# Expert weights of a two-layer mixture-of-experts kernel: fourteen places of 1 MB filled by a table, in place of a ring of seven places of 2 MB

## The chip, the cores and the metric

The kernel runs on 1 core of one Trainium2 chip. The metric is the device time of one execution in microseconds (us); three runs of the kernel before gave 3231.19 us in the median. A core has a matrix engine (TensorE, PE in the profile), a vector engine (DVE), a scalar engine (ACT), GpSimd (POOL), and a sync engine (SP) that here only waits and issues DMAs; 16 DMA engines carry what any of them issues.

## The reference, cut to what matters

Two transformer blocks follow each other over 1024 tokens of width 1024, all in float32. Each ends in a mixture of experts: 32 experts, every token goes to 2, each expert has three weight matrices of 2 MB.

```python
def expert_block(args):
    xb, e = args
    return (jax.nn.silu(xb @ w_gate[e]) * (xb @ w_up[e])) @ w_down[e]
```

`w_gate[e]` and `w_up[e]` are 1024x512, `w_down[e]` is 512x1024. The outputs are weighted by the router and summed per token. Everything else (attention of two kinds, gating, norms) is not touched by the change, apart from renamed semaphores.

## The kernel before, in words

The kernel is written engine by engine: one Python function per stage and engine, and semaphores between them. The two expert stages are the calls with L = 0 and L = 1 of `sync_experts`, `tensor_experts` and their siblings.

**Blocks.** The kernel sorts the tokens of a layer by expert and the experts by load, and has a fixed plan: `PROFILE` says how many rows the expert of each rank gets at most, `ORDER` in which order the ranks come. Class `Plan` (L1389) makes a list of blocks of 64 or 32 rows out of it. An expert has one to four blocks: in layer 0 there are 51 blocks (37 of 64 rows and 14 of 32), in layer 1 46 (36 and 10). Positions 0, 6 and 17 of layer 0 and position 16 of layer 1 have four blocks of 64 rows; positions 10 and 21 of layer 0 and 3 and 11 of layer 1 have three. 31 experts stand in the plan; whatever overflows goes through a hardware loop (`sync_loop`, `tensor_loop`), which here runs once in each layer, ahead of position 27 in layer 0 and 26 in layer 1.

**Weights.** SP loads `w_gate`, `w_up` and `w_down` of one expert after the other, in one DMA of 2 MB each (`load_expert`, L1763 and L1766). Load number n goes into place n % 7 (`RING`), seven places of 2 MB in SBUF. Before it issues, SP waits (`freed`) until the last block of the expert that held the place is through its product: `p_gu` counts the blocks whose gate and up products are done, `p_dn` those whose down product is done. SP works strictly in this order; a load that waits holds back all behind it. A load of gate or up brings 16 KB in one piece to each of 128 partitions, a load of down four pieces of 4 KB.

**Products.** For block b TensorE does four of the eight steps kk of the gate and up products (L1667), then the transposes of the hidden rows of block b - 1 (L1622) and of the next tokens (L1613), then the other four steps (L1667 again), then the down product of block b - 1 (L1640). So the down product of an expert's last block comes behind the gate and up products of the next expert's first block. At an expert's first block it waits for gate and up together (`weight`), at its first down product for down.

Beside the weights the DMA engines carry, for each block, the token rows that GpSimd gathers (`rows_in`) and the output rows that it stores (`rows_out`).

Of the kernel before, what the change touches and what calls it, by code (L numbers as in the profile page):

```python
# [85 lines left out]
class Shared:  # L86
# [7 lines left out]
    "d_gate d_attn d_q0 d_q1 d_row d_rowb d_dil d_norm0 d_norm1 d_post "  # L94
    "a_cond v_acc p_col v_mod "
    "a_sq v_rstd v_xn p_tr v_tr a_tr "
    "z_q p_in v_in a_in "
    "v_ln a_ln p_ws v_ws p_sv "
# [3 lines left out]
    "d_zero d_wr d_xn0 d_xn1 p_lg v_rt a_rt p_cnt p_tab "  # L102
    "d_e0 d_e1 d_e2 d_e3 d_e4 d_e5 d_e6 d_xt0 d_xt1 d_xt2 d_xt3 d_xt4 d_ys0 d_ys1 d_ys2 d_ys3 d_ys4 d_ys5 "
    "p_xt v_xt a_xt p_gu a_sg v_h p_ht v_ht p_dn v_yb v_gh "
# [390 lines left out]
def vector_gate(k):  # L495
    V, s = k.nc.vector, k.s
# [20 lines left out]
    V.wait_ge(s["p_ws"].sem, 1)  # L517
# [3 lines left out]
    for m in range(NT):  # L521
        V.wait_ge(s["p_sv"].sem, m + 1)
# [21 lines left out]
def tensor_gate_weights(k):  # L544
# [5 lines left out]
    i_.then_inc(*s["p_ws"].up())  # L550
# [66 lines left out]
def sync_attn(k):  # L617
    Q, s, A = k.nc.sync, k.s, k.A
    v = attn_views(k)
    d = s["d_attn"]  # L620
    Q.wait_ge(s["v_ws"].sem, 17)
    Q.wait_ge(s["p_sv"].sem, 8)
# [9 lines left out]
def vector_attn(k):  # L632
# [3 lines left out]
    V.wait_ge(s["p_sv"].sem, 8)  # L636
    V.memset(v.relp, 0.0).then_inc(*pr.up())
    V.wait_ge(s["d_attn"].sem, 400)
# [58 lines left out]
def scalar_attn(k):  # L697
# [4 lines left out]
    S.wait_ge(s["p_sv"].sem, 8)  # L702
# [432 lines left out]
def vector_route(k, L, scale, bias, biased):  # L1135
# [82 lines left out]
    V.wait_ge(s["p_cnt"].sem, L + 1)  # L1218
# [66 lines left out]
    V.wait_ge(s["p_tab"].sem, L + 1)  # L1285
# [35 lines left out]
def tensor_route(k, L):  # L1321
# [34 lines left out]
    i_.then_inc(*s["p_tab"].up())  # L1356
# [27 lines left out]
RING = 7  # L1384
# [7 lines left out]
class Plan:  # L1392
# [3 lines left out]
    def __init__(self, profile, firsts, before):  # L1396
# [25 lines left out]
        self.loop_at = tuple((3 * self.loop_q + j) % RING for j in range(3))  # L1422
        self.b0, self.t0, self.w0 = (0, 0, [0] * RING) if before is None else (
            before.b0 + len(before.blocks), before.t0 + len(before.tiles),
            [before.loads(u, 10 ** 9) for u in range(RING)])

    def number(self, q, j):


        return 3 * (q + (q >= self.loop_q)) + j  # L1430

    def loads(self, u, n):

        return self.w0[u] + len([m for m in range(u, 96, RING) if m <= n and m // 3 != self.loop_q])

# [11 lines left out]
def expert_views(k):  # L1447
    v = Shared()
    ring = [k.R2[:, 4096 * u:4096 * u + 4096] for u in range(4)]
    ring += [k.R0[:, 4096 * u:4096 * u + 4096] for u in range(2)]  # L1450
    ring.append(k.R1[:, 0:4096])
    v.flat = ring
    v.up = [r.rearrange("p (k n) -> p k n", k=8) for r in ring]
    v.down = [r.rearrange("p (k n) -> p k n", k=4) for r in ring]
# [146 lines left out]
def tensor_experts(k, L):  # L1601
# [14 lines left out]
    def hidden_T(b):  # L1616
# [4 lines left out]
        for kk in range(P.blocks[b].rows // 16):  # L1621
            i_ = T.transpose(k.ps[:, hidden_bank(b), 64 * kk:64 * kk + 64], v.hb[:, 128 * kk:128 * kk + 128],  # L1622
                             k.ident[0:64, 0:64])
# [144 lines left out]

# [975 lines left out]
```

## Time and profile before

| | us |
|---|---|
| median of 3 runs | 3231.19 (3224.49 to 3260.21) |
| span of the profiled execution | 3229.6 |
| PE busy | 2768.7 (86%) |
| DVE, ACT, POOL busy | 1130.5, 646.7, 304.5 |
| chain that ended last: PE | 74% |
| chain that ended last: DMA | 13%, of it the load of w_up 8% and of w_down 2% |
| bytes by DMA | 605.18 MB, mean 187 GB/s |

The chain is followed back from the last instruction, at each step to what released it. Busy is the time in which an engine executes; the share of DMA in a window is the mean over the 16 engines. The first expert stage lies between 934 and 1622 us of the span, the second between 2540 and 3180 us.

### The profile page before, as it was taken

Reading aid. Unit: us, or ns where it says so; the run is one execution under the profiler, and the core shown is the slowest. Engines: PE = TensorE matmul, PEld = TensorE weight load, DVE = VectorE, ACT = ScalarE, POOL = GpSimd, SP = SyncE. Lnnn points to the kernel's source line nnn. Section 1 sums busy time; section 2 is a strip of 40 time slices with the busy share of each in tenths; the row PEclk is TensorE's granted clock in tenths of the full one; section 3 lists DMA queues with packets and bytes.
Section 4 is the critical chain, followed back from the end, with each engine's and each line's share of the span. In section 5 each row is a group of like instructions: output and inputs, shape, how many; then the busy total and the mean of one; then the engine's idle time right before and its main releaser. Section 6 shows DMA issues by size and latency. Waiting matters only on the chain.

```text
span 3229.6 us, 34694 instructions
## 1 busy us (share of the span) xinstructions
PE 2768.7 (86%) x13500; PEld 1352.3 (42%) x13500; DVE 1130.5 (35%) x2847; ACT 646.7 (20%) x1603; POOL 304.5 (9%) x395
## 2 busy tenths in 40 slices
PE   3999999998949878978659999999998489888972
PEld 2456844444443333333224444555564433333421
DVE  4225724337462112211160002777723612111214
ACT  3115600000111101100041001555612111111101
POOL 0000000000001101111020000222500111111102
PEclk9999999999969989989879999999989689989996
DMA  7221014227156988899952100000000699898997
GB/s 272 104 72 53 2 52 156 86 97 247 42 221 232 353 330 333 305 343 370 352 194 97 52 26 1 27 27 28 26 2 20 231 340 385 309 369 304 369 388 276
DMA packets 193830, 605.18 MB, mean 187 GB/s; under 512 B 53122, under 2 KB 95618, under 8 KB 177156
## 3 DMA queue, kind: packets, MB, share of 16 engines
q1 hardware_dynamic: 137076, 531.35, 43.6%
q0 software_dynamic: 56592, 71.62, 6.9%
q8 instruction: 108, 1.77, 0.2%
q14 instruction: 54, 0.44, 0.0%
HBM read 554.65 MB, written 47.98 MB: 187 GB/s over the span
## 4 chain that ended last, share of the span: by engine, by line
PE 74%; DMA 13%; DVE 9%; issue 2%; ACT 1%; SPq 0%; POOL 0%; DVEq 0%; POOLq 0%; ACTq 0%
PE ps L1667 17%; DMA R<-in_w_up 8%; PE ps L1640 7%; PE ps L928 7%; PE ps L2184 6%; PE ps L2616 3%; PE ps L2181 3%; PE ps L433 3%; PE ps L932 3%; PE ps L1046 3%; PE ps L439 2%; DMA R<-in_w_down 2%; PE ps L2425 2%; PE ps L1613 2%; PE ps L2429 1%
## 5 line engine op out<-in xcount | busy, mean ns | idle before, releaser
L1667 PE MATMUL ps<-R 128*64 128x512 f32 (+1 forms) x3872 | 675.4, 549 | 151.6 <-DMA R<-in_w_up 110.0
L1667 PEld LDWEIGHTS ps<-R 128*64 128x64 f32 (+1 forms) x3872 | 221.9, 135 | 525.1 <-issue 490.9
L1640 PE MATMUL ps<-R 128*64 128x512 f32 (+1 forms) x1936 | 309.7, 509 | 2.2 <-DVE R L1504 2.2
L928 PE MATMUL ps<-R 128*128 128x512 f32 x512 | 227.5, 604 | 0.5 <-ACT R L723 0.5
L1567 ACT ACTIVATE R<-ps,small 128x64 f32<-128x64 f32 (+1 forms) x256 | 87.3, 421 | 684.2 <-PE ps L1613 684.2
L2184 PE MATMUL ps<-R 128*128 128x512 f32 x512 | 220.5, 592 | 1.6 <-DVE R L2006 1.6
L1504 DVE COPY R<-ps 128x256 f32<-128x256 f32 (+1 forms) x97 | 37.9, 391 | 450.2 <-PE ps L1622 450.2
L1640 PEld LDWEIGHTS ps<-R 128*64 128x64 f32 (+1 forms) x1936 | 106.3, 126 | 189.1 <-issue 171.7
L1532 DVE TENSOR_TENSOR R<-ps,R 64x512 f32<-64x512 f32 (+1 forms) x97 | 59.8, 617 | 313.7 <-PE ps L1667 201.2
L928 PEld LDWEIGHTS ps<-R 128*128 128x128 f32 x512 | 98.8, 194 | 124.5 <-issue 123.8
L2184 PEld LDWEIGHTS ps<-R 128*128 128x128 f32 x512 | 97.0, 190 | 122.8 <-issue 121.0
L1581 ACT ACTIVATE R<-ps 64x512 f32<-64x512 f32 (+1 forms) x97 | 52.5, 541 | 472.8 <-PE ps L1667 472.7
L1692 POOL DMA_INDIRECT R<-XN,xidx x52 | 52.3, 1006 | 812.5 <-DVE R L1292 794.2
L1046 PE MATMUL ps<-R 128*128 128x512 f32 x256 | 116.3, 617 | 0.0
L2616 PE MATMUL ps<-R 128*128 128x512 f32 x256 | 113.0, 604 | 0.4 <-DVE R L2303 0.4
L433 PE MATMUL ps<-R 128*128 128x512 f32 x256 | 110.2, 592 | 0.0
L2181 PE MATMUL ps<-R 128*128 128x512 f32 x256 | 110.2, 592 | 0.0
L887 DVE TENSOR_TENSOR XR<-ps,XR 128x512 f32<-128x512 f32 x32 | 22.0, 691 | 214.0 <-PE ps L932 214.0
L1495 DVE TENSOR_SCALAR R<-ps,small 128x64 f32<-128x64 f32 (+1 forms) x256 | 75.9, 359 | 40.7 <-PE ps L1613 40.0
L1699 POOL DMA_DIRECT2D YE<-R x49 | 39.4, 805 | 522.1 <-DVE R L1516 504.2
L2425 PE MATMUL ps<-R,cst 128*128 128x512 f32 (+3 forms) x192 | 80.5, 501 | 1.4 <-DVE R L2340 1.4
L905 ACT ACTIVATE XR<-ps 128x512 f32<-128x512 f32 x32 | 19.1, 597 | 309.1 <-PE ps L928 309.1
(320 smaller groups left out, 3586.9 us busy)
## 6 DMA issues: line engine op xcount, KB each, us to landing
R<-in_w_gate SPq DMA_DIRECT2D x64, 2048.0 KB, 17.5
R<-in_w_up SPq DMA_DIRECT2D x64, 2048.0 KB, 18.4
R<-in_w_down SPq DMA_DIRECT2D x64, 2048.0 KB, 24.7
R<-in_w_ada SPq DMA_DIRECT2D x40, 1024.0 KB, 5.4
R<-in_w_in SPq DMA_DIRECT2D x13, 2048.0 KB, 9.2
YE<-R POOLq DMA_DIRECT2D x41, 256.0 KB, 21.7
R<-in_w_ada SPq DMA_DIRECT2D x4, 2048.0 KB, 16.4
XR<-in_x SPq DMA_DIRECT2D x16, 512.0 KB, 11.5
```

The lines of the kernel that those rows point to most:

```text
L433: i_ = T.matmul(k.ps[:, b, :], wv[:, kk, 128 * a:128 * a + 128], toks, start=kk == 0, stop=kk == 7)
L928: i_ = T.matmul(o, wv[:, kk, cols], k.hT[:, kk, tk], start=kk == 0, stop=kk == 7)
L932: i_ = T.matmul(o, w4[:, g, cols], x4[:, g, tk], start=g == 0, stop=g == 3)
L1046: i_ = T.matmul(k.ps[:, n % 6, :], lhsT[:, m, 128 * i:128 * i + 128], wv[:, m, :], start=m == 0, stop=m == 7)
L1495: i_ = V.tensor_scalar(v.xT[t % 2][:, kk, 0:n], k.ps[:, 2, 128 * kk:128 * kk + n], scale[:, kk:kk + 1], bias[:, kk:kk + 1], ALU.mult, ALU.add)
L1567: i_ = S.activation(v.xT[t % 2][:, 4 + kk, 0:n], k.ps[:, 3, 128 * kk:128 * kk + n], ACT.Identity, scale=scale[:, 4 + kk:5 + kk], bias=bias ...
L1640: i_ = T.matmul(k.ps[r * j:r * j + r, 5 + b % 2, 0:n], v.hT[b % 2][:, c:c + r], v.down[m][:, kk, n * j:n * j + n], start=kk == 0, stop=kk ...
L1667: i_ = T.matmul(k.ps[P0 + r * j:P0 + r * j + r, b % 2, 0:n], x_, w[:, kk, n * j:n * j + n], start=kk == 0, stop=kk == 7)
L2181: i_ = T.matmul(k.ps[:, second_bank(n), :], k.hT[:, kk, 128 * x:128 * x + 128], wv[:, kk, :], start=kk == 0, stop=kk == 7)
L2184: i_ = T.matmul(k.ps[:, second_bank(n), :], wv[:, kk, 128 * x:128 * x + 128], k.hT[:, kk, 512 * hf:512 * hf + 512], start=kk == 0, stop=kk ...
L2425: i_ = T.matmul(z, k.C("nge"), lp[:, 0:N], start=False, stop=first and not diag, skip_group_check=True)
L2616: i_ = T.matmul(k.ps[:, 2 * (n % 3) + a, :], v.oT[a][:, c, 128 * i:128 * i + 128], w[4 * a + c][:, 512 * h2:512 * h2 + 512], start=c == 0, ...
```

## The change

Each weight matrix is cut into two halves of 1 MB, and SBUF holds them in 14 places (`HOMES`) that fill the same bytes as the seven did. An expert has six parts, loaded as gate and up of the first half (parts 0, 1), gate and up of the second half (2, 3), and the two halves of down (4, 5). A half of gate or up holds the rows of four of the eight steps kk, a half of down those of two of its four; each half is 8 KB in one piece to each partition. Which place a part takes is fixed when the program is built: `products` lists the order of the products, and `place_pieces` gives each part the place whose present content is used up first by that list. A new semaphore `p_g0` counts the blocks whose first four steps of gate and up are done.

```diff
+    def place_pieces(self):
+        last = {what: n for n, what in enumerate(self.products())}
...
+        for q in names:
+            for part in range(6):
+                u = min(range(HOMES), key=lambda u: (until[u], u))
+                self.home[q, part], self.held[q, part] = u, held[u]
+                held[u], until[u] = (q, part), last[q, (0, 0, 1, 1, 2, 2)[part]]
```

```diff
-    def freed(n):
-
-        q, j = (n - RING) // 3, (n - RING) % 3
-        if n >= RING and q != P.loop_q:
-            q -= q > P.loop_q
-            Q.wait_ge(s["p_dn" if j == 2 else "p_gu"].sem, P.b0 + P.ends[q])
+    def freed(q, part):
+        if P.held[q, part] is not None:
+            q0, part0 = P.held[q, part]
+            if q0 != "loop":
+                Q.wait_ge(s[("p_g0", "p_g0", "p_gu", "p_gu", "p_dn", "p_dn")[part0]].sem, P.b0 + P.ends[q0])
...
+def load_piece(k, part, weights, e_r, place, sem, by):
+    w, half = (weights[part % 2], part // 2) if part < 4 else (weights[2], part - 4)
+    src = w.rearrange("e (p k) n -> e p (k n)", p=128)[:, :, 2048 * half:2048 * half + 2048]
+    k.nc.sync.dma_start(place, src[bass.ds(e_r, 1), :, :].rearrange("o p n -> (o p) n")).then_inc(sem, by)
```

Since down is now loaded with rows 4p to 4p+3 on partition p (so that a half is one piece), the hidden values have to come in the same order. For blocks of 64 rows the transposes of the hidden rows read every fourth element; for blocks of 32 rows the gate and up products read their weights two elements of each four, and the transposes every second element.

```diff
-            if first:
-                weight(P.number(q, 0))
-                weight(P.number(q, 1))
...
             for kk in range(8):
+                hf = kk // 4
                 if kk == 4:
                     if b > begin:
                         hidden_T(b - 1)
                     if off == 0 and t + 1 < tiles:
                         turn(t + 1)
+                if first and kk % 4 == 0:
+                    weight(q, 2 * hf)
+                    weight(q, 2 * hf + 1)
...
+                if kk == 3:
+                    i_.then_inc(*s["p_g0"].up())
...
+    def hidden_columns(w, r, j):
+        if r == 64:
+            return w
+        return w.rearrange("q (p k) -> q p k", k=4)[:, :, 2 * j:2 * j + 2]
```

The down product waits for its second half at its third step. The loop takes six parts where it took three matrices, and still waits for all of them. Some semaphores are merged to make room for fourteen; the waits on them are for the same events.

SP's queue in layer 0 where the loads of the experts at positions 8 and 9 stand; the names behind "waits" are semaphores. Before:

```order
L1763 ISA [waits p_dn]
L1763 DMA R<-in_w_gate 128x4096
L1763 DMA R<-in_w_up 128x4096 [waits p_gu]
L1766 DMA R<-in_w_down 128x4x1024 [waits p_gu]
L1747 TENSOR_LOAD eid
L1747 ISA x2
L1763 ISA [waits p_dn]
L1763 DMA R<-in_w_gate 128x4096
L1763 DMA R<-in_w_up 128x4096 [waits p_gu]
L1766 DMA R<-in_w_down 128x4x1024 [waits p_gu]
```

The same place of the changed kernel, all of position 8 and the first loads of position 9:

```order
L1800 ISA [waits p_dn]
L1800 DMA R<-in_w_gate 128x2048
L1800 DMA R<-in_w_up 128x2048 [waits p_dn]
L1800 ISA [waits p_g0]
L1800 DMA R<-in_w_gate 128x2048
L1800 DMA R<-in_w_up 128x2048 [waits p_g0]
L1800 DMA R<-in_w_down 128x2048 [waits p_gu] x2
L1782 TENSOR_LOAD eid
L1782 ISA x2
L1800 ISA [waits p_g0]
L1800 DMA R<-in_w_gate 128x2048
L1800 DMA R<-in_w_up 128x2048 [waits p_g0]
```

At position 8 the parts behind the first two waited for `p_gu` of position 6 (four blocks) and now the first pair waits for its `p_g0`; at position 9 the first loads waited for `p_dn` of position 6 and now wait for `p_g0` of position 7.

TensorE's queue at the start of the expert stage of layer 0, position 0; `d_e...` are the semaphores of the weight places. Before:

```order
L1667 MATMUL ps<-R 64x512 [waits d_e0,d_e1,a_xt,v_xt]
L1667 MATMUL ps<-R 64x512 x7
L1613 MATMUL ps<-cst,R 128x128 [waits v_xt,d_xt1]
L1613 MATMUL ps<-cst,R 128x128 x3
L1613 MATMUL ps<-cst,R 128x128 [waits a_xt]
L1613 MATMUL ps<-cst,R 128x128 x3
L1667 MATMUL ps<-R 64x512 x16
L1622 MATMUL ps<-cst,R 128x64 [waits v_h]
L1622 MATMUL ps<-cst,R 128x64 x3
L1667 MATMUL ps<-R 64x512 x8
```

And after:

```order
L1700 MATMUL ps<-R 64x512 [waits d_e0,d_e1,a_xt,v_xt]
L1700 MATMUL ps<-R 64x512 x7
L1633 MATMUL ps<-cst,R 128x128 [waits v_xt,d_xt1]
L1633 MATMUL ps<-cst,R 128x128 x3
L1633 MATMUL ps<-cst,R 128x128 [waits a_xt]
L1633 MATMUL ps<-cst,R 128x128 x3
L1700 MATMUL ps<-R 64x512 [waits d_e3,d_e2]
L1700 MATMUL ps<-R 64x512 x15
L1644 MATMUL ps<-cst,R 128x64 [waits v_h]
L1644 MATMUL ps<-cst,R 128x64 x3
L1700 MATMUL ps<-R 64x512 x8
```

No product moves; the first wait is for 2 MB (two halves) where it was for 4 MB, and a second wait stands in the middle of the first block.

## Rows read from the trace of the kernel before

**Rows 1.** Windows, the two expert stages: busy us of each engine, PE clock, DMA share, GB/s
```profile
934.00:1622.00 688.00, 564.30 (x3640) 228.16 (x3644) 146.12 (x366) 73.15 (x181) 75.29 (x87) 0.90 0.87 328
2540.00:3180.00 640.00, 534.65 (x3200) 212.43 (x3200) 139.25 (x352) 70.40 (x176) 71.72 (x83) 0.90 0.94 350
```

**Rows 2.** Waits of PE, 934 to 1622 us: total, times, longest
```profile
PE ps L1667 <- DMA R<-in_w_up: 48.2, 8, 13.2
PE ps L1667 <- issue: 31.3, 6, 7.7
```

**Rows 3.** Waits of PE, 2540 to 3180 us
```profile
PE ps L1667 <- DMA R<-in_w_up: 61.8, 13, 8.4
```

**Rows 4.** Timeline of SP (start, us): first three issues, then positions 8 and 9
```profile
934.07 0.36 SPq L1763 DMA_DIRECT2D R<-in_w_gate  x1
934.53 0.38 SPq L1763 DMA_DIRECT2D R<-in_w_up  x1
935.00 0.38 SPq L1766 DMA_DIRECT2D R<-in_w_down  x1
...
1140.62 0.33 SPq L1763 DMA_DIRECT2D R<-in_w_up  x1
1141.04 0.38 SPq L1766 DMA_DIRECT2D R<-in_w_down  x1
1155.93 0.34 SPq L1763 DMA_DIRECT2D R<-in_w_gate  x1
```

**Rows 5.** Timeline of PE, end of position 6 and start of position 7
```profile
1136.54 0.46 PE L1622 MATMUL ps<-cst,R 64*128 64x64 f32 x4
1136.92 3.65 PE L1667 MATMUL ps<-R 128*64 128x512 f32 x16
1140.40 3.60 PE L1640 MATMUL ps<-R 128*64 128x512 f32 x16
1143.84 3.60 PE L1667 MATMUL ps<-R 128*64 128x512 f32 x16
```

**Rows 6.** Windows, dips of DMA behind experts of four blocks
```profile
978.00:1013.00 35.00, 35.00 (x174) 12.48 (x172) 6.49 (x13) 4.80 (x9) 2.70 (x3) 1.00 0.22 56
1129.00:1143.00 14.00, 14.00 (x70) 4.70 (x68) 2.48 (x4) 1.19 (x2) 0.84 (x1) 1.00 0.22 59
1358.00:1374.00 16.00, 16.00 (x78) 5.40 (x76) 2.48 (x4) 1.80 (x5) 0.84 (x1) 1.00 0.26 69
2903.00:2924.00 21.00, 21.00 (x106) 7.68 (x104) 4.70 (x10) 2.48 (x6) 2.60 (x3) 1.00 0.22 56
```

**Rows 7.** Windows, smaller dips, first and last of nine, and layer 0's end
```profile
1217.00:1225.00 8.00, 8.00 (x45) 3.28 (x43) 2.21 (x6) 1.89 (x5) 0.41 (x1) 1.00 0.40 104
...
2936.00:2940.00 4.00, 4.00 (x20) 1.29 (x18) 0.69 (x1) 0.00 (x0) 1.40 (x2) 1.00 0.53 151
...
1594.00:1600.00 6.00, 6.00 (x64) 2.51 (x64) 1.80 (x3) 0.35 (x1) 0.80 (x1) 1.00 0.50 137
```

**Rows 8.** Windows, full stretches between the dips
```profile
1042.00:1132.00 90.00, 81.27 (x538) 32.59 (x535) 18.39 (x43) 11.22 (x28) 9.46 (x11) 0.96 0.94 353
1240.00:1361.00 121.00, 107.83 (x644) 42.02 (x642) 23.78 (x56) 14.70 (x38) 14.04 (x16) 0.93 0.98 370
2940.00:3150.00 210.00, 181.89 (x1144) 71.31 (x1142) 42.11 (x102) 24.12 (x61) 20.01 (x25) 0.94 1.00 381
```

**Rows 9.** One line: landing of position 0's gate and up, then its down
```profile
DMA to landing us min/median/max: 8.1/10.3/12.6
...
DMA to landing us min/median/max: 17.2/17.2/17.2
```

**Rows 10.** Groups by form: products of 32-row blocks, and weight loads of transposes
```profile
L1667 PE MATMUL ps<-R 128*32 128x256 f32 x1536 | 105.7, 422 | 38.8 <-issue 35.3 <-DMA R<-in_w_up 2.0 <-DVE R L1495 1.5
L1613 PEld LDWEIGHTS ps<-cst,R 64*128 64x128 f32 x280 | 33.7, 200 | 13.6 <-DMA R<-XN,xidx 10.0 <-issue 3.6
L1622 PEld LDWEIGHTS ps<-cst,R 64*128 64x128 f32 x340 | 28.7, 140 | 71.3 <-issue 70.8 <-DVE R L1532 0.5
```

More of the change, by code:

```diff
@@ L1421, in __init__, with products @@
         self.loop_q = min(q for q in starts if q >= 26)
[L1422 to L1434, printed above, removed]
+        self.b0, self.t0, self.w0 = (0, 0, [0] * HOMES) if before is None else (
+            before.b0 + len(before.blocks), before.t0 + len(before.tiles), before.filled)
+        self.place_pieces()
+    def products(self):
+        B, n = self.ends[self.loop_q - 1], len(self.blocks)
+        out = []
+        for begin, end in ((0, B), (B, n)):
+            for b in range(begin, end):
+                out += [(self.blocks[b].q, ph) for ph in (0, 1)]
+                if b > begin:
+                    out += [(self.blocks[b - 1].q, ph) for ph in (2,)]
+            out += [(self.blocks[end - 1].q, ph) for ph in (2,)]
+            if end == B:
+                out += [("loop", ph) for ph in range(3)]
+        return out
+    def place_pieces(self):
+        last = {what: n for n, what in enumerate(self.products())}
+        names = list(range(len(self.order)))
+        names.insert(self.loop_q, "loop")
+        held, until, self.filled = [None] * HOMES, [-1] * HOMES, list(self.w0)
+        self.home, self.nth, self.held = {}, {}, {}
+        for q in names:
[3 more added lines that the diff above has]
+                held[u], until[u] = (q, part), last[q, (0, 0, 1, 1, 2, 2)[part]]
+                if q != "loop":
+                    self.filled[u] += 1
+                    self.nth[q, part] = self.filled[u]
 PROFILE = ((23, 12, 6, 5, 5, 3, 3), (27, 11, 5, 3, 3, 1, 1))
@@ L1619, in hidden_T, with weight @@
             T.wait_ge(s["v_ht"].sem, P.b0 + b - 1)
[L1621 to L1623 removed]
+        n = P.blocks[b].rows // 16
+        h = v.hb[:, 0:128 * n].rearrange("r (p k) -> r k p", k=n)
+        for kk in range(n):
+            i_ = T.transpose(k.ps[:, hidden_bank(b), 64 * kk:64 * kk + 64], h[:, kk, :], k.ident[0:64, 0:64])
         i_.then_inc(*s["p_ht"].up())
[L1626 to L1627 removed]
+    def weight(q, part):
+        T.wait_ge(s[f"d_e{P.home[q, part]}"].sem, 16 * P.nth[q, part])
     def down(b):
         row = P.blocks[b]
[L1631 removed]
+        n, r = 8 * row.rows, row.rows
         T.wait_ge(s["v_ht"].sem, P.b0 + b + 1)
[L1633 to L1634 removed]
         if b >= 2:
@@ L1788, in sync_loop @@
         Q.wait_ge(o["pe"], j * 4 + 4)
-        for i, w in enumerate((wg_d, wu_d, wd_d)):
-            load_expert(k, i, w, e_r, v.flat[P.loop_at[i]], o["w"], 16)
+        for part in range(6):
+            load_piece(k, part, (wg_d, wu_d, wd_d), e_r, v.flat[P.home["loop", part]], o["w"], 16)
 def sync_loop_done(k, L):
```

114 lines of the change are left out of this document (54 added, 60 removed).

## The prediction, made before the changed kernel ran

> **What bounds the kernel now.** I read first the chain that ended last on the page (PE 74%, DMA 13%, nearly all of it weight loads), then the windows of the two expert stages, then who waits for whom inside them, and last the timelines of SP and PE at one expert of four blocks.
>
> The expert stages take 688 and 640 us of 3229.6 [rows 1]. In each, PE is busy for 564 and 535 us, and the DMA engines for 87% and 94%. Each stage loads 96 matrices of 2 MB (31 experts and one turn of the loop), 201.3 MB. Neither engine is idle for lack of work: each waits at times for the other. PE waits for gate and up (48.2 us in 8 waits and 31.3 in 6 that are put down to issue in layer 0, 61.8 us in 13 in layer 1) [rows 2, 3]. Between these waits there are stretches in which PE is busy without a gap and DMA is nearly idle: in 1129 to 1143 us PE is busy 14.00 of 14 us and the DMA share is 0.22 [rows 6]. There all seven places hold weights that PE still needs.
>
> The cause is seen in SP's queue. Position 8's up and down wait for position 6, an expert of four blocks. They are issued at 1140.62 and 1141.04 [rows 4], just when PE ends the last gate and up products of position 6 (they start at 1136.92, the down product follows at 1140.40) [rows 5]. The next load, gate of position 9, goes at 1155.93 [rows 4]: it waits for the down product of position 6's last block, which in PE's order stands behind the first block of position 7. Two loads take about 10 us (below), so DMA runs dry a second time, for a few us.
>
> In the full stretches DMA moves 353 to 381 GB/s at a share of 0.94 to 1.00 [rows 8]. So the time of a stage is the bytes at that rate plus the dips, and the change can only win what lies in the dips. I weigh a dip as its length times (1 - share). The four behind experts of four blocks: 35 x 0.78 = 27.3, 14 x 0.78 = 10.9, 16 x 0.74 = 11.8, 21 x 0.78 = 16.4 us [rows 6]. Nine smaller ones, 3 to 11 us long, add up to 25.4 us by the same rule, the first of them 8 x 0.60 = 4.8, the last 4 x 0.47 = 1.9 [rows 7]. Together 91.8 us.
>
> **The change part by part.** *Earlier release.* The bytes in SBUF are the same, so a dip does not close by more room, only by places that come free sooner. The first halves of gate and up are free after four of the eight steps of the last block. That is one transpose group and four steps sooner: 1140.57 - 1136.54 = 4.0 us [rows 5]. Loading 2 MB into these two places takes about 5 us, by which time the second halves are free. So each of the four large dips shrinks by 4.0 us.
>
> *Earlier start.* An expert starts when 2 MB of it have landed instead of 4 MB. The second half lands about 5 us later; meanwhile PE does four steps (3.60 us) and the transposes (0.46, often more with the next tokens) [rows 5]. Where PE had been waiting for the expert's weights it is then 4 to 5 us further; I take 4.4. An expert of four blocks is released that much sooner. It holds for three of the four large dips (PE waited at the start of those experts; before the first, at 978 us, it did not). Large dips: 4.0 for the first, 3 x (4.0 + 4.4) = 25.2 for the others.
>
> *Order by last use.* At position 9 the first pair now waits for `p_g0` of position 7, whose four steps run 1143.84 to 1147.4 [rows 5], instead of 1155.9: 8.5 us sooner, so the second, short dip is gone. The small dips are of this kind, or stand behind experts of three blocks and are under 6.5 us each, less than 4.0 + 4.4. I close all: 25.4 us. At the end of layer 0 the last expert's loads wait for a down product too; 1594 to 1600 us has a share of 0.50 [rows 7]: 3.0 us. Layer 1 has no such dip.
>
> *Full stretches.* 1042 to 1132 us has only 0.94, where 1240 to 1361 has 0.98 [rows 8]; short holes of the same sort are in it. 90 x 0.04 = 3.6 us.
>
> *Costs.* SP issues 384 loads instead of 192, at 0.33 to 0.38 us each [rows 4]: six for an expert are 2.3 us, hidden behind the 15 us that its 6 MB take; uncovered it would be 192 x 0.38 = 73 us. The speed of 8 KB pieces the trace does not show. Gate landed 8.1 us after 934.07, up 12.6 after 934.53, down 17.2 after 935.00 [rows 4, 9], thus at 942.2, 947.1 and 952.2: 4.9 us for 2 MB in pieces of 16 KB, 5.1 in pieces of 4 KB. Bounds: all at the 4 KB pace costs 128 x 0.2 = 26 us, all at the 16 KB pace gains 64 x 0.2 = 13 us. 8 KB lies between; I take 0. The hidden transposes read with a step now. The transposes of the tokens, which read with a step of eight, have weight loads of 200 ns, those of the hidden rows 140 [rows 10]: 60 ns on 340 loads is 20 us if nothing hides it, nothing if each hides behind its predecessor. One load exposed per block is 97 x 0.06 = 6 us; about half falls where PE waits anyhow: 3 us. In the 24 blocks of 32 rows the gate and up products read two of each four elements. No matmul here streams like that. Lower bound 0; upper, the factor 200/140 on their 105.7 us [rows 10], 45 us. They sit mostly in small experts, where PE waits for weights, so I take 0.
>
> The Trainium skill (SBUF — State Buffer, "Door 1: The DMA port swizzle") says that reads keep full bandwidth with at least two accesses to each 16-byte line. Two floats of four is just that, so by the page this term is 0; no run so far shows it.
>
> **Sum.** 4.0 + 25.2 + 25.4 + 3.0 + 3.6 - 3 = 58 us. The profiled execution's 3229.6 becomes 3171.6; the median of the runs lies 1.6 us above it, so 3173.
>
> **The rivals.** *All idle closes.* Against it: the 37 us left of the large dips by my sum (23.3 + 2.5 + 3.4 + 8.0) exist because SBUF holds 14 MB, and a four-block expert keeps PE for about 4 x 11.3 = 45 us (0.46 + 3.65 + 3.60 + 3.60 for a block [rows 5]). For it: PE's head start may add up over several experts, and down may gain from larger pieces. All dips closed is 91.8 + 6.6 = 98 us, with the 13 above 111: 3120 to 3135.
>
> *Half the gain is given back.* The pieces run at the 4 KB pace (26 us), or the 32-row blocks slow PE where it has no slack (up to 45 us): 3173 + 26 = 3199, with part of the other 3215. The first row speaks for it (a measurable 0.2 us), the position of the small experts against the second.
>
> *Slower: a queued load has a fixed cost.* If each of the 192 added loads kept the engines idle for x us, the stages grow by 192x. It decides from 58/192 = 0.30 us; at 0.47 us the kernel is 1% slower; at 0.6 it takes 3173 + 115 = 3288. A lone load shows 8.1 us against 4.9 for the next in the queue, so 3.2 us of fixed cost exist [rows 9], but they hide behind the load ahead: three loads queued together land 4.9 and 5.1 us apart, at over 410 GB/s. The share of 1.00 over 210 us [rows 8] leaves no room for idling between loads of 2 MB.
>
> The Trainium skill (DMA: Bandwidth & Descriptors, "Anatomy of one DMA") fits a GpSimd-issued DMA as 2.0 us plus bytes at 436 GB/s. Paid in full for each added load that would be 384 us and some 3557 us in all. The queued loads above contradict it for SP's: 2 MB would take 6.8 us by it, and 4.9 is seen.
>
> *No effect.* The stages could be bound by DMA alone, the dips made up for elsewhere. Then a dip would not matter; but behind each one PE waits again for weights within two experts, so it does. I count this with the second rival.
>
> **How the numbers follow.** My forecast 0.60, with its own range 3150 to 3190; all closed 0.14; gain half given back or lost 0.20; slower by a fixed cost 0.06. A change of 1% (32 us) is about what a measurement of this kernel can tell from none; it lies at 3199 and 3263. Faster by over 1%: 0.60 + 0.14 + half of 0.20 = 0.84. Slower by over 1%: 0.04. Within: 0.12. The range takes in most of the first rival and the 4 KB pace with a little of the reads: 3130 to 3205.
>
> **What would show it.** In the changed profile the window behind the first expert of four blocks should still show a dip of about 23 us, the other three 2 to 8, and the small ones none; the stages should take about 650 and 622 us. SP should issue the first pair behind a four-block expert about 4 us ahead of the end of its last gate and up products. PE's wait for weights in both stages falls from 141 us to some 90, in more and shorter waits. Products of 32-row blocks should keep 422 ns. I am wrong if the DMA share in full stretches stays near 1 at under 350 GB/s (pieces too small), if the matmuls of 32-row blocks grow, or if the dips stay as they are.

## The result, and the profile after

The changed kernel takes 3160.72 us in the median of four runs (3159.37 to 3164.46), the kernel before 3232.23 (3224.49 to 3260.21): a ratio of 0.9757, 95% interval 0.972 to 0.9793. The prediction was 3173 in a range of 3130 to 3205, and faster. The profiled execution's span fell from 3229.6 to 3163.3 us.

First the windows of the changed kernel: the two expert stages, the four dips behind experts of four blocks, and full stretches between them. The columns are those of [rows 1], [rows 6] and [rows 8].

```profile
931.60:1571.20 639.60, 562.61 (x3644) 234.72 (x3644) 146.09 (x366) 73.14 (x181) 75.30 (x87) 0.93 0.94 353
2506.40:3113.20 606.80, 530.65 (x3200) 220.86 (x3200) 139.06 (x353) 70.39 (x176) 71.54 (x82) 0.93 0.99 369
978.00:1009.00 31.00, 31.00 (x152) 11.61 (x150) 5.80 (x12) 3.41 (x8) 2.70 (x3) 1.00 0.20 59
1119.00:1127.00 8.00, 8.00 (x42) 2.84 (x40) 1.12 (x2) 0.00 (x0) 0.84 (x1) 1.00 0.46 135
1331.00:1339.00 8.00, 8.00 (x40) 2.90 (x38) 1.12 (x2) 0.00 (x0) 0.84 (x1) 1.00 0.37 91
2854.00:2863.00 9.00, 9.00 (x46) 3.27 (x44) 1.80 (x3) 0.59 (x1) 0.84 (x1) 1.00 0.21 41
1037.00:1120.00 83.00, 83.00 (x546) 33.76 (x544) 18.43 (x44) 11.22 (x28) 11.24 (x13) 1.00 0.99 368
1127.00:1331.00 204.00, 188.90 (x1178) 77.47 (x1176) 42.84 (x100) 26.22 (x66) 25.35 (x29) 0.97 1.01 377
2863.00:3100.00 237.00, 215.51 (x1340) 86.67 (x1340) 48.63 (x115) 26.98 (x68) 24.84 (x30) 0.94 1.01 385
```

PE is about as busy as before (563 and 531 us), but the stages are shorter, and the DMA share is 0.94 and 0.99 instead of 0.87 and 0.94 [rows 1]. By length times (1 - share) the four dips are 24.8, 4.3, 5.0 and 7.1 us. In the stretches between them the share is 0.99 to 1.01 (1339 to 1563 us and 2520 to 2854 us too), so the nine smaller dips of before are all but gone.

That PE's busy time hardly moved hides two changes of its work. Groups by form of the gate and up products of 64-row blocks and of the hidden transposes, first in the kernel before, then in the changed one:

```profile
L1667 PE MATMUL ps<-R 128*64 128x512 f32 x2336 | 569.7, 633 | 112.7 <-DMA R<-in_w_up 108.0 <-DVE R L1495 3.1 <-issue 1.7
L1622 PE MATMUL ps<-cst,R 64*128 64x64 f32 x340 | 42.1, 239 | 0.0
...
L1700 PE MATMUL ps<-R 128*64 128x512 f32 x2336 | 546.5, 611 | 52.2 <-DMA R<-in_w_up 47.4 <-DVE R L1515 3.1 <-issue 1.7
L1644 PE MATMUL ps<-cst,R 64*128 64x64 f32 x340 | 61.2, 295 | 0.0
```

The transposes take 19.1 us more. The same gate and up products take 23.2 us less, with those of the 32-row blocks (below) 25.6. The products are the same; what differs is the granted clock behind PE's waits. In the kernel before, around one wait:

```profile
1245.87 3.60 PE L1640 MATMUL ps<-R 128*64 128x512 f32 x16
1253.24 5.35 PE L1667 MATMUL ps<-R 128*64 128x512 f32 x16 [3.77 <-DMA R<-in_w_up]
1260.00 3.65 PE L1667 MATMUL ps<-R 128*64 128x512 f32 x16
```

PE stood idle for 3.77 us, and the first half of the next products took 5.35 us instead of 3.6; the granted clock was 0.60 from 1253.2 to 1256.7 us, and 1.00 ahead of the wait (1245 to 1249 us) and again from 1260. So a wait costs its length and often another 1.3 to 3 us. The changed kernel has fewer long waits, and its granted clock in the stages is 0.93 instead of 0.90. The prediction had no term for this.

PE's waits for weights, first in layer 0, then in layer 1 (total, times, longest); `L1869` is the product that waits for down inside the loop:

```profile
PE ps L1700 <- DMA R<-in_w_up: 25.8, 7, 9.1
PE ps L1869 <- DMA R<-in_w_down: 17.8, 1, 17.8
PE ps L1700 <- issue: 1.7, 1, 1.7
...
PE ps L1700 <- DMA R<-in_w_up: 35.2, 13, 7.5
```

The waits for gate and up are 25.8 + 1.7 + 35.2 = 62.7 us in 21 waits, where before they were 141.3 in 27 [rows 2, 3], and in layer 1 another 5.7 put down to issue. The prediction said some 90 us, in more and shorter waits; they are less than that, and fewer.

SP's timeline around the second four-block expert (position 6): the last load ahead of the dip, then the three groups that it waited for, and the first pair of position 9.

```profile
1097.08 0.34 SPq L1800 DMA_DIRECT2D R<-in_w_gate  x1
1097.52 0.38 SPq L1800 DMA_DIRECT2D R<-in_w_up  x1
1123.53 0.33 SPq L1800 DMA_DIRECT2D R<-in_w_gate  x1
1123.95 0.46 SPq L1800 DMA_DIRECT2D R<-in_w_up  x1
1127.60 0.85 SPq L1800 DMA_DIRECT2D R<-in_w_down  x2
1134.61 0.34 SPq L1800 DMA_DIRECT2D R<-in_w_gate  x1
```

PE's timeline at the same place, the end of position 6:

```profile
1119.75 3.60 PE L1700 MATMUL ps<-R 128*64 128x512 f32 x16
1123.28 0.69 PE L1644 MATMUL ps<-cst,R 64*128 64x64 f32 x4
1123.90 3.65 PE L1700 MATMUL ps<-R 128*64 128x512 f32 x16
```

The pair goes at 1123.53, when the first four steps are done, and the second half ends at 1127.55: 4.0 us of lead, as forecast. The next expert's first loads go at 1134.61, 7.0 us behind down, where before they went 14.9 us behind it (1155.93 after 1141.04, [rows 4]). The four hidden transposes take 0.69 us, where they took 0.46 [rows 5]. By form, the products of 32-row blocks and the weight loads of the hidden transposes are:

```profile
L1700 PE MATMUL ps<-R 128*32 128x256 f32 x1536 | 103.3, 411 | 15.2 <-DMA R<-in_w_up 13.7 <-DVE R L1515 1.5
...
L1644 PEld LDWEIGHTS ps<-cst,R 64*128 64x128 f32 x340 | 47.9, 208 | 69.3 <-issue 68.9 <-DVE R L1552 0.4
```

**Outside the stages.** One difference between the two executions is none of the change's. The router of layer 1, between the stages, ran at a granted clock of 0.50 in the profiled execution of the changed kernel:

```profile
2445.00:2479.00 34.00, 34.00 (x163) 33.69 (x163) 15.94 (x44) 10.63 (x29) 0.00 (x0) 0.50 0.31 124
```

In that of the kernel before, the same stage had 0.89:

```profile
2495.00:2516.00 21.00, 20.60 (x166) 20.32 (x167) 15.88 (x45) 10.91 (x30) 0.00 (x0) 0.89 0.50 201
```

0.50 is TensorE's lower level, 1.2 GHz. In the fourteen traces of the table below, the stretch between the stages takes either 917 or 935 us and the one ahead of the first stage 930 to 934 or 946 to 949 us. Both values are found with kernels like the one before (917 in e5, 935 in e9) and with kernels like the changed one (917 in e1, 935 in e4), though both traces of the changed kernel itself have 935. So I compare the kernels by the two expert stages, each from SP's first issue of a gate to its issue of `final_g` behind the last expert. The changed kernel was profiled a second time to see how far that can be trusted. Each ratio is to the runs of the kernel before in the same group of runs; their medians are 3243.40 us for e1 to e4, 3239.53 for a0 and e5 to e7, 3231.47 for e8 to e10 and 3232.82 for e11.

| kernel (label) | layer 0 | layer 1 | both stages | between | median, us | ratio to before, 95% |
|---|---|---|---|---|---|---|
| before | 688.4 | 639.3 | 1327.7 | 917.4 | 3232.23 | |
| changed | 639.6 | 606.7 | 1246.3 | 935.2 | 3160.72 | 0.9757 (0.972 to 0.9793) |
| a0_changed_again | 638.5 | 608.8 | 1247.2 | 935.3 | 3160.02 | 0.9742 (0.9711 to 0.9774) |
| e1_ring14 | 669.7 | 629.0 | 1298.8 | 917.0 | 3204.98 | 0.9892 (0.9856 to 0.9928) |
| e2_no_early_release | 656.4 | 614.9 | 1271.3 | 917.1 | 3173.87 | 0.9802 (0.9745 to 0.9859) |
| e3_no_early_start | 660.1 | 627.6 | 1287.7 | 917.3 | 3198.44 | 0.9871 (0.9806 to 0.9935) |
| e4_pieces_only | 697.8 | 641.5 | 1339.3 | 935.1 | 3257.55 | 1.0045 (1.0016 to 1.0075) |
| e5_before_down_pk | 677.4 | 622.5 | 1299.9 | 917.0 | 3215.54 | 0.9931 (0.9895 to 0.9967) |
| e6_down_kp | 644.6 | 613.1 | 1257.7 | 916.7 | 3170.33 | 0.9793 (0.9759 to 0.9827) |
| e7_double_dmas | 890.8 | 888.9 | 1779.7 | 935.4 | 3713.32 | 1.1483 (1.1432 to 1.1533) |
| e8_down_row_halves | 634.9 | 604.8 | 1239.7 | 917.0 | 3160.5 | 0.9768 (0.9718 to 0.9818) |
| e9_2mb_8kb_pieces | 696.1 | 646.1 | 1342.2 | 934.7 | 3255.67 | 1.0048 (1.0018 to 1.0077) |
| e10_table_of_seven | 665.0 | 622.9 | 1287.9 | 935.0 | 3203.03 | 0.9879 (0.9819 to 0.9939) |
| e11_mixed_loads | 651.9 | 596.9 | 1248.9 | 917.0 | 3163.41 | 0.9767 (0.9734 to 0.9801) |

Two traces of the changed kernel differ by 0.9 us in the stages, while their spans differ by 16.6 (3163.3 and 3179.9). In the profiled pair the stages lost 81.4 us, the part between them gave 17.8 back, and the start and the end won 2.8: 66.3 of span up to rounding.

### The profile page after: what moved, and what is told of

Read it like the earlier page. It is cut to its first block, busy times and chain, and to the rows that moved or that the text cites. A ratio compares the mean times of both kernels' runs of the same rounds, so it can differ in the third digit from the quotient of the medians.

```text
span 3163.3 us, 35208 instructions
## 1 busy us (share of the span) xinstructions
PE 2780.4 (88%) x13500; PEld 1384.2 (44%) x13500; DVE 1131.2 (36%) x2847; ACT 646.9 (20%) x1603; POOL 304.7 (10%) x395
## 4 chain that ended last, share of the span: by engine, by line
PE 76%; DMA 12%; DVE 9%; issue 2%; ACT 1%; SPq 1%; POOL 0%; DVEq 0%; POOLq 0%; ACTq 0%
PE ps L1700 16%; DMA R<-in_w_up 8%; PE ps L928 7%; PE ps L1662 7%; PE ps L2216 7%; PE ps L2648 4%; PE ps L2213 3%; PE ps L433 3%; PE ps L932 3%; PE ps L1046 3%; PE ps L439 2%; PE ps L2457 2%; DMA R<-in_w_down 2%; PE ps L1633 2%; PE ps L2461 1%
## 5 line engine op out<-in xcount | busy, mean ns | idle before, releaser
L1700 PE MATMUL ps<-R 128*64 128x512 f32 (+1 forms) x3872 | 649.8, 532 | 67.3 <-DMA R<-in_w_up 61.1
L1662 PE MATMUL ps<-R 128*64 128x512 f32 (+1 forms) x1936 | 311.4, 511 | 1.7 <-DVE R L1524 1.7
L928 PEld LDWEIGHTS ps<-R 128*128 128x128 f32 x512 | 98.8, 194 | 124.5 <-issue 123.8
L905 ACT ACTIVATE XR<-ps 128x512 f32<-128x512 f32 x32 | 19.1, 597 | 309.1 <-PE ps L928 309.1
```

The costliest lines, as they stand in the source:

```text
L928: i_ = T.matmul(o, wv[:, kk, cols], k.hT[:, kk, tk], start=kk == 0, stop=kk == 7)
L1662: i_ = T.matmul(k.ps[r * j:r * j + r, 5 + b % 2, 0:n], v.hT[b % 2][:, c:c + r], w[:, kk % 2, n * j:n * j + n], start=kk == 0, stop=kk == 3)
L1700: i_ = T.matmul(hidden_out(k.ps[P0 + r * j:P0 + r * j + r, b % 2, 0:n], r), x_, hidden_columns(w, r, j), start=kk == 0, stop=kk == 7)
```

## The experiments

**The three mechanisms, each undone, then all three.** They are the order by last use (a ring of fourteen again), the early release of the first halves, and the early start.

```diff
-                u = min(range(HOMES), key=lambda u: (until[u], u))
+                u = (6 * names.index(q) + part) % HOMES
```

> The changed kernel with its fourteen places filled in turn (load number n into place n % 14), everything else as changed: halves, early release, early start. Theory: the order by last use closes the short dip behind each large expert and part of the small ones, since the first pair of an expert waits again for a down product (p_dn). Without it 10 to 25 us of the small dips come back: about 3178 us. Rival (the order is worth nothing, the finer release alone closes the dips): 3161 us, as the changed kernel.

The stages take 52 us more than those of the changed kernel, where 10 to 25 were expected. Windows of position 6's dip and of a second one behind it:

```profile
1124.00:1136.00 12.00, 12.00 (x58) 4.20 (x56) 1.85 (x4) 1.27 (x4) 0.84 (x1) 1.00 0.33 98
1147.00:1155.00 8.00, 8.00 (x62) 2.80 (x58) 1.45 (x3) 1.30 (x4) 0.56 (x1) 1.00 0.30 82
```

And SP's issues there:

```profile
1133.97 0.33 SPq L1800 DMA_DIRECT2D R<-in_w_gate  x1
1134.40 0.45 SPq L1800 DMA_DIRECT2D R<-in_w_up  x1
1138.05 0.85 SPq L1800 DMA_DIRECT2D R<-in_w_down  x2
1153.59 0.34 SPq L1800 DMA_DIRECT2D R<-in_w_gate  x1
```

With the ring the gate of position 9 again waits for the down product of position 6: it goes 15.5 us behind down instead of 7.0, and DMA falls dry a second time. The mechanism of the prediction is seen; its price is nearly twice the 28 us of the prediction.

```diff
-                Q.wait_ge(s[("p_g0", "p_g0", "p_gu", "p_gu", "p_dn", "p_dn")[part0]].sem, P.b0 + P.ends[q0])
+                Q.wait_ge(s[("p_gu", "p_gu", "p_gu", "p_gu", "p_dn", "p_dn")[part0]].sem, P.b0 + P.ends[q0])
```

> The changed kernel, but the first halves of gate and up are released only when all eight steps are done (p_gu in place of p_g0). Theory: each of the four large dips is 4.0 us longer again, and some of the small ones open by as much: 16 to 30 us, about 3181 us. Rival (release matters little because the loads behind it are landed in time anyway): 3161 us.

25 us more in the stages, within the 16 to 30 expected; in the medians it is 13.

```diff
-                if first and kk % 4 == 0:
-                    weight(q, 2 * hf)
-                    weight(q, 2 * hf + 1)
+                if first and kk == 0:
+                    for part in range(4):
+                        weight(q, part)
```

> The changed kernel, but TensorE waits for all four halves of gate and up before it starts an expert. Theory: three large dips are 4.4 us longer again and PE is later at every expert where it waits for weights: 13 to 25 us, about 3180 us. Rival (the head start is only lent, since PE waits for the second half then): 3161 us.

41 us more, where 13 to 25 were expected, and PE's waits for gate and up are 97.1 us (42.4 + 1.7 + 53.0), 34 more than with the early start.

> All three taken back at once: fourteen places in turn, release by whole matrices, start with all of gate and up. What is left of the change is the size of the loads and the layout of down with its stepped transposes. Theory: the dips are those of the kernel before; down in larger pieces gives back up to 13 us, the slower transposes (0.69 us for four, 0.46 before) take up to 22: 3225 to 3240 us. Rival (smaller loads as such are the gain): near 3161 us.

With all three undone (the three edits together), the loads by halves alone are slower than the kernel before: by 0.45% in time, by 11.6 us in the stages. The median of 3257.55 lies above the 3225 to 3240 expected. So the whole gain comes from the three mechanisms, 93 us in the stages. Of these 93, PE's busy time gives 30 (1123.4 us in e4, 1093.3 in the changed kernel), all of it in the gate and up products (679.7 against 649.8 us), which run at the lower clock less often; the other 63 are idle time of PE. The single values add up to 118, more than the three together: each mechanism is worth more when the other two are there, so that undoing one also takes away part of what they give.

> The changed kernel once more, as the measure for the others of this group. 3161 us, within 3. In its profile the router stage of layer 1 ran at a granted clock of 0.50 where the kernel before had 0.89; if that belongs to the kernel, it is seen again; if it is chance of the execution, it may be gone and the span is then about 15 us shorter.

The median is as expected (3160.02). The router of layer 1 ran at the lower clock again (935.3 us between the stages), so the span did not get shorter; it is longer, since the part ahead of the first stage took 946.6 us instead of 931.6. The 0.9 us in the stages (1.1 less in layer 0, 2.1 more in layer 1) are the only measure of their scatter, from two traces.

**What the loads cost: layout, number, size of the pieces.** First the layout of down alone, in the kernel before: rows 4p to 4p+3 on partition p, so one piece of 16 KB instead of four of 4 KB, with the transposes and the 32-row products that read with a step. Ring, 2 MB loads and waits stay.

```diff
-        src = w.rearrange("e (k p) n -> e p k n", p=128)
+    src = w.rearrange("e (p k) n -> e p (k n)", p=128)
```

> The kernel before (seven places of 2 MB) with the layout of down alone changed: rows 4p to 4p+3 on partition p, 16 KB in one piece, and so the transposes and the 32-row products that read with a step. Theory: down lands in 4.9 us where it took 5.1 (up to 13 us less in the stages), each block's hidden transposes take 0.23 us longer (97 blocks, 22 us, about half of it where PE waits anyway): 3225 to 3245 us. Rival (the layout is a gain of its own, since 4 KB pieces slow the full stretches): 3205 us or less.

3215.54 lies between the two expectations: 28 us less in the stages than the kernel before, in spite of the slower transposes. And the reverse in the changed kernel, down in 4 KB pieces and no steps:

```diff
-        h = v.hb[:, 0:128 * n].rearrange("r (p k) -> r k p", k=n)
...
+        src = weights[2].rearrange("e (k p) n -> e p k n", p=128)[:, :, 2 * part - 8:2 * part - 6, :]
```

> The changed kernel with the old layout of down: a half is two pieces of 4 KB to each partition, and nothing reads with a step (hidden transposes and 32-row products as before the change). Theory: the transposes of a block take 0.46 us again instead of 0.69, 22 us less of PE work, of which some 10 on the path; down lands at 5.1 us for 2 MB instead of 4.9, up to 13 us more where DMA is the limit. About 3158 us, between 3148 and 3168. Rival (large pieces are what keeps the full stretches full): 3175 us or more.

The hidden transposes' weight loads have 138 ns again:

```profile
L1643 PEld LDWEIGHTS ps<-cst,R 64*128 64x128 f32 x340 | 28.4, 138 | 69.1 <-issue 68.7 <-DVE R L1552 0.4
```

But the stages take 11 us more, and 3170.33 lies between the two expectations: the 4 KB pieces cost more than the steps.

e4 and e5 have the same layout, ring order and releases, and differ in the loads: 384 of 1 MB in 8 KB pieces against 192 of 2 MB in 16 KB (and in that e4's down product waits for its halves one by one). e4 takes 39 us more. The next kernel tells number from size: e5's 192 loads, but each place is two runs of columns, so that six of seven loads come in 8 KB pieces.

```diff
-    ring = [k.R2[:, 4096 * u:4096 * u + 4096] for u in range(4)]
...
+    for r, n in ((k.R2, 4), (k.R0, 2), (k.R1, 1)):
+        two = r[:, 0:4096 * n].rearrange("p (h u n) -> p h u n", h=2, u=n)
+        ring += [two[:, :, u, :] for u in range(n)]
```

> The kernel before with down in the order of the changed kernel (as in e5_before_down_pk: loads of 2 MB, ring of seven), but each place split into two runs of columns, so that six of seven loads write two pieces of 8 KB to each partition instead of one of 16 KB. Number of loads, order and waits stay. e4_pieces_only, with 1 MB loads of 8 KB pieces, took 39 us more in the two stages than e5. Theory 'size of the pieces': 6/7 of the 39 us come, stages of 1333 us (1328 to 1339), the kernel 3249. Rival 'number of loads': nothing comes, stages of 1300 us (1296 to 1304), the kernel 3216.

42 us more than e5, as much as e4 and 3 above the range of the theory. It is the size of the pieces; 192 more DMAs cost nothing that these runs can tell. The page's row for SP's DMA queue (packets, MB, share of the 16 engines' span) shows the same, in this order of kernels: e5, then e9, then e4, then the changed one, then the one before.

```profile
q1 hardware_dynamic: 112500, 531.35, 42.7%
```
```profile
q1 hardware_dynamic: 133748, 531.35, 43.0%
```
```profile
q1 hardware_dynamic: 140148, 531.36, 43.1%
```
```profile
q1 hardware_dynamic: 140148, 531.36, 44.6%
```
```profile
q1 hardware_dynamic: 137076, 531.35, 43.6%
```

Share times span (3213.4, 3259.7, 3257.2, 3163.3, 3229.6) is the time in which the engines work on the same bytes: 1372, 1402, 1404, 1411 and 1408 us, each known to about 2 us since the share is rounded. Pieces of 8 KB cost some 30 us over those of 16 KB. The kernel before, with a third of its weights in 4 KB pieces and the rest in 16 KB, pays the same 36. So the change moved gate and up to smaller pieces and down to larger ones, and in DMA time the two cancel within 3 us, which is all that the rounding lets one tell.

An attempt to price an added load directly: every half in two DMAs of 64 partitions each.

```diff
+    for P0 in (0, 64):
+        k.nc.sync.dma_start(place[P0:P0 + 64, :], flat[P0:P0 + 64, :]).then_inc(sem, 16)
```

> The changed kernel with each half loaded by two DMAs of 0.5 MB (partitions 0 to 63 and 64 to 127), 768 loads for 384, the pieces still 8 KB. Theory (a queued load has no cost of its own on the DMA engines): 3161 us within 6; SP issues twelve loads for an expert in 4.6 us, still less than the 15 us they take. Rival (a fixed cost x for each queued load): 384 x longer, 3276 us at 0.3 us.

Both expectations are missed by far, and the page's slices say why (DMA share in tenths, and GB/s):

```profile
DMA  6220043361799999999850100010029999999998
GB/s 236 91 82 28 23 141 107 102 217 47 180 230 241 253 258 294 242 245 267 261 205 23 46 0 24 24 35 14 0 68 230 240 254 310 324 212 239 240 239 247
```

The engines are full at some 240 GB/s; over the two stages it is 253 at shares of 1.01 and 0.99. It is not idle time between loads but a lower rate. The run changed two things, half of the partitions for each load and 0.5 MB instead of 1; that the half of the partitions is the cause is argued, from e4 and e9, where the size and number of loads did nothing. So this run says nothing on the fixed cost. That question is answered by e9 and e4: 1342.2 us with 192 loads, 1339.3 with 384.

**The steps in the transposes.** Halves of down cut by rows 0 to 255 and 256 to 511 are still 8 KB to a partition, but the hidden transposes then read every second float, and the 32-row products read without a step.

```diff
-        h = v.hb[:, 0:128 * n].rearrange("r (p k) -> r k p", k=n)
+        h = v.hb[:, 0:128 * n].rearrange("r (h p k) -> r h k p", h=n // 2, k=2)
...
+        src = weights[2].rearrange("e (h p k) n -> e h p (k n)", h=2, p=128)[:, part - 4, :, :]
```

> The changed kernel, with the halves of down cut by rows 0 to 255 and 256 to 511 (still 8 KB in one piece to each partition), so that the hidden transposes read every second float instead of every fourth and the 32-row products read their weights without a step. Theory: the weight loads of the hidden transposes took 208 ns instead of 140 because of the step of four floats, and a step of two is as fast as none: a block's four transposes take about 0.46 us again instead of 0.69, 97 x 0.23 = 22 us less of PE, of which half shows, since the other half lies where PE waits for weights: the two stages take 1236 us (1230 to 1242) where the changed kernel took 1246 to 1247, the kernel 3150. Rival: any step costs the same, the transposes stay at 0.69 us and the stages at 1247, the kernel at 3161.

Groups by form:

```profile
L1644 PEld LDWEIGHTS ps<-cst,R 64*128 64x128 f32 x340 | 47.9, 209 | 69.1 <-issue 69.1
L1699 PE MATMUL ps<-R 128*32 128x256 f32 x1536 | 98.9, 401 | 13.0 <-DMA R<-in_w_up 11.5 <-DVE R L1515 1.5
```

A step of two costs as much as one of four (209 ns), and the theory falls. The stages are 6.6 us shorter nonetheless, so that their 1239.7 us lie in the theory's range by luck: the gain is in the 32-row products, which read without a step, and PE is busy for 7 us less. In the runs' medians nothing is to be seen of it (3160.5).

The mean of these products (401 ns here, 411 in the changed kernel, 422 in the one before) mixes the two clocks, so it does not give the price of the step. Single halves of a block do. First two of the kernel before, at a granted clock of 1.00 and, behind a wait, of 0.50; then one of the changed kernel, at 1.00:

```profile
1286.94 1.93 PE L1667 MATMUL ps<-R 128*32 128x256 f32 x32
1402.33 3.64 PE L1667 MATMUL ps<-R 128*32 128x256 f32 x32 [6.66 <-issue]
1254.12 2.02 PE L1700 MATMUL ps<-R 128*32 128x256 f32 x32
```

At the upper clock it is 1.93 us without a step, in e6 and e8 too, and 2.02 with two floats of four: 0.09 us, some 4 us over the 48 halves of the 24 blocks.

**Towards a faster kernel.** The table of last use with seven places of 2 MB and whole matrices, so 16 KB pieces:

```diff
-HOMES = 14
+HOMES = 7
...
-                held[u], until[u] = (q, part), last[q, (0, 0, 1, 1, 2, 2)[part]]
+                held[u], until[u] = (q, part), last[q, (1, 1, 2)[part]]
```

> The changed kernel with seven places of 2 MB and whole matrices in loads of 2 MB (16 KB pieces), placed by the table of last use; no early release and no early start by halves. So it is e5_before_down_pk with the table in place of the ring. Theory: the order by last use is worth what it was worth in the changed kernel (52 us in the stages), and the 39 us that the halves cost are not paid: 1300 - 50 = 1250 us in the stages (1243 to 1262), the kernel 3165. Rival: the order needs small places to be worth that much (with seven places only the small dips close, 25 us): 1275 us or more, the kernel 3190.

The theory falls: against e5, which has the ring, the table wins 12 us, not 50. Behind the three-block expert at position 10 there is still a dip:

```profile
1196.00:1208.00 12.00, 12.00 (x62) 4.79 (x60) 2.90 (x7) 1.93 (x6) 1.77 (x2) 1.00 0.50 181
```

With whole matrices an expert waits for all of gate and up, and gives both back at once. A reading that fits is that the table needs small places, or the early start and release that come with them, to have something to choose from; no run here separates these.

The last kernel mixes: down always whole in two neighbouring places, gate and up whole for some experts. The text below speaks of 40 of 62; it was 29, and the other 33 kept halves.

```diff
+WHOLE = (((0, 2), (1, 3), (4, 5)), ((0,), (1,), (2,), (3,), (4, 5)))
+                at = min(range(0, HOMES, n), key=lambda u: (max(until[u:u + n]), u))
```

> The changed kernel with whole matrices where halves gain little: every down is one load of 2 MB (16 KB pieces) into two neighbouring places, and 40 of 62 experts also load gate and up whole; the other 22 (around the experts of several blocks) keep halves of gate and up. The table of last use, the early release of each half and the waits by halves stay. Theory (the size of the pieces costs 0.1 us per MB, 39 us over 384 MB, while small places and halves matter only where SBUF runs full): stages of 1226 us (1218 to 1238) where the changed kernel took 1246, the kernel 3140. Rival (what makes the changed kernel fast is that every place is small; pairs of places come free late, as with seven places, where the table was worth only 12 us): stages of 1255 us or more, the kernel 3170.

Stages of the mixed kernel:

```profile
948.00:1599.90 651.90, 565.63 (x3644) 233.81 (x3644) 146.04 (x366) 73.15 (x181) 75.33 (x87) 0.92 0.91 346
2516.90:3113.80 596.90, 529.10 (x3200) 217.89 (x3200) 138.82 (x352) 70.40 (x176) 71.57 (x82) 0.93 0.99 375
```

1248.9 us, between the theory and the rival. Layer 1 is 10 us shorter than in the changed kernel: DMA is full there (0.99), so it ends sooner when the engines work faster (375 against 369 GB/s). Layer 0 is 12 us longer, at a share of 0.91 instead of 0.94; it has three of the four experts of four blocks, and pairs of places come free later, which would explain it but was not tested. No kernel tried beats the changed one by more than its runs scatter; a mix in layer 1 and halves in layer 0 would be the next to try, and was not.

## Why the prediction was right, and where its terms were not

**The mechanism** held at each place. The dips behind the four-block experts were forecast at 23.3, 2.5, 3.4 and 8.0 us and are 24.8, 4.3, 5.0 and 7.1; the small ones are gone; SP issues 4.0 us ahead of the end of the last gate and up products; the bytes stayed. The stretch of short holes that the sum counted at 3.6 us (0.94 at 1042 to 1132 us) is at 0.99 (1037 to 1120 us). e4, with halves and none of the three mechanisms, shows that nothing else made the kernel faster.

**The size of the gain was too low.** The forecast for the stages was 650 and 622 us; they take 639.6 and 606.7. Gains of 61 us (the sum without its costs) were forecast, and e4 against the changed kernel gives 93. Term by term, what undoing one part costs in the stages (in the presence of the other two, which is why the three add up to more than 93; the reasons given are arguments, no run isolates them):

- Order by last use: 28 us forecast (25.4 and 3.0), 52 measured. I closed only the holes visible as nine dips. The ring's second wait behind every large expert probably also made the expert after it late, and so the places that this one gives back.
- Early start: 13 us forecast (3 x 4.4), 41 measured. It was credited only to the three four-block experts that PE had waited for. PE waits for gate and up about twenty times in the two stages; the start by halves can shorten each of these waits (62.7 us against 97.1 without it), and whatever PE does sooner releases a place sooner.
- Early release: 16 us forecast (4 x 4.0), 25 measured; every expert releases early, not only the large ones.

Two things were sized too low. The first is what the dips hold, which I counted by eye. Cutting the stages of the kernel before, each without its last 15 us or so, in which the last loads land, into windows of 2 us and adding up length times (1 - share) where the share is under 0.75 gives 123.8 us, not the 91.8 that I summed from picked windows. In the changed kernel the same sum is 54.6 us, where the forecast left 37: 69 us closed, where the sum had 61. Over the whole stages, at every share, the rows of the two stages give 128 us before [rows 1] and 44 after, enough for all of the 81 us. The same gain is seen from PE's side: it is idle for less time, and its products behind waits run less often at the lower clock. That clock is the second thing, and the sum had it at nothing without a reason: against the changed kernel the gate and up products take 30 us more in e4, 18 in e1, 10.5 in e3 and 9 in e2, inside the 93, 52, 41 and 25 us of the stages.

**The costs were too low as well.** 3 us were forecast; e4 is 11.6 us slower in the stages than the kernel before, with the same DMA time (1404 and 1408 us). The forecast exposed one weight load of the transposes per block and hid half of these. In fact nearly all of the four is exposed: 0.69 - 0.46 = 0.23 us for a block of 64 rows, of 4 x 0.068 that the loads grew, and over all blocks the transposes keep PE busy for 19.1 us more. That is the 20 us that the prediction named for the case that nothing hides it. How much of the 11.6 us is theirs no run isolates, since e6 undoes them together with the pieces.

**The pieces.** The term was 0 with bounds of +26 and -13, and in sum it is right: 1408 us of engine time before, 1411 after. But it is right as a difference of two terms of some 30 us. e5 shows what I judged at 13 us at most: down in 16 KB instead of 4 KB pieces wins 28 us in the stages even with the slower transposes. The landings of the first three loads [rows 9], 4.9 and 5.1 us apart, understated it: 0.2 us for 2 MB, while 1408 - 1372 = 36 us over 64 loads is 0.56 us.

**The 32-row products** take 411 ns in the mean, less than the 422 of before [rows 10], but that is the clock. At the same clock the step costs 2.02 against 1.93 us for half a block, some 4 us in all where the forecast took 0 and had 45 as its upper bound. The Trainium skill (SBUF — State Buffer, "Door 1: The DMA port swizzle"), by which two accesses to each 16-byte line keep the full bandwidth, comes within these 5% for the products. It does not carry over to weight loads: 209 ns with every second float, against 138 without a step.

**The rivals.** *All idle closes*: the four large dips alone still hold 41 us, so no. *Half the gain is given back*: no, the pieces cost nothing in sum, and the 32-row blocks 4 us. *A fixed cost per queued load*: e4 and e9 exclude it, 384 and 192 loads with stages 3 us apart, the fewer loads even longer. The fit cited from the Trainium skill (DMA: Bandwidth & Descriptors, "Anatomy of one DMA") is for DMAs issued by GpSimd; its 2.0 us are not paid by SP's loads in the queue, where 192 of them would be 384 us.

**The total** came nearer to the forecast than its parts, and in that there is luck. The stages beat their forecast, 81.4 us against 58, because the gains were too low by 32 us and the costs by 9, and in the profiled execution 17.8 us were given back between the stages, 13 of them in the router windows above, at the lower clock, which no step of the prediction had. In the medians the gain is 71.5 us against the 58 forecast.

## What to carry to other kernels

When a stage is bound now by one engine and now by the other, measure the idle time of the DMA queue in fine, even windows over the whole stage, and credit a change of release or start times to every place where one waits, not only to the largest dips. Count a wait of TensorE at more than its length, since the products behind it can run at the lower clock; and before comparing the mean times of a product in two kernels, look at single ones at the same granted clock. Filling places in the order of last use was worth 52 us with fourteen small places and 12 with seven large ones. Weigh the smaller pieces against it: for these weights 16 KB to a partition instead of 8 KB is worth some 2% of the DMA time, and the smaller ones cost 39 and 42 us of the stages in the kernels with a ring (e4 and e9 against e5).

## What the runs showed of the hardware

- The same 201 MB of weights in each stage take more engine time in smaller pieces: for all that SP's queue carries 1372 us with 16 KB to a partition, 1402 to 1411 with 8 KB; the number of DMAs (192 or 384) did not matter.
- Loads of 0.5 MB that write 64 partitions at a time kept the 16 engines at a share near 1 with only some 250 GB/s, where those over 128 partitions reach 370 to 385. The stages grew from 1246 to 1780 us.
- The weight load of a transpose whose source is read with a step of two, four or eight floats takes 209, 208 and 200 ns (the last in [rows 10]), without a step 138 to 140; TensorE shows nearly all of it, 0.69 us for four transposes instead of 0.46. For a matmul's moving operand, two floats of four cost 5% at the same clock, 2.02 us for 1.93.
- Behind a wait for weights of 3.77 us the granted clock was 0.60 for 3.5 us, and products that take 3.65 us at 1.00 took 5.35; behind one of 6.66 us it was 0.50 (TensorE's lower level), and 1.93 us became 3.64. With fewer such waits the gate and up products of the two stages take 26 us less in the changed kernel than in the one before.
- The router's code between the stages, the same in all kernels, ran at a granted clock of 0.89 in the trace of the kernel before and at 0.50 in that of the changed one; the stretch took 917 us in eight traces and 935 in six, 18 us that the change did not make.
